# Two indexer heads as two row tiles, and scores, top-k and modulation panels in one stage

## What is computed

```python
def dsa_attend(q, iq, iw, qpos, k, v, ik, kpos, n_sel):
    dots = jnp.einsum('bqhd,bsd->bqhs', iq.astype(f32), ik.astype(f32))
    score = jnp.einsum('bqhs,bqh->bqs', jax.nn.relu(dots), iw.astype(f32))
    score = jnp.where(causal[None], score, -jnp.inf)
    top_score, idx = lax.top_k(score, n_sel)
    ...
def adaln(c, w, b):
    m = jax.nn.silu(c) @ w + b
    return jnp.split(m[:, None, :], 6, axis=-1)
```

## Time and profile before

| | |
|---|---|
| median of 3 runs | 1914.38 us (1914.14 to 1914.92) |
| the profiled execution | 1902.81 us |
| its span, first to last instruction | 1901.0 us |
| mean granted TensorE clock | 0.892 |
| TensorE busy | 1682.0 us (88%) |
| VectorE, ACT, POOL busy | 803.3 (42%), 682.4 (36%), 149.2 (8%) |
| the stages from the scores to the top-k's end | 157 to 303.4 us |

### The profile page before, as it was taken

One profiled execution on the slowest core, in us unless ns is written; L12 is line 12 of the kernel. 1 busy time (PEld: TensorE's weight loads), 2 busy tenths in 40 slices (PEclk: granted clock), 3 DMA queues, 4 the chain that ended last, 5 costly groups with the idle time before them and its releaser, 6 DMA issues.

```text
span 1901.0 us, 31118 instructions
## 1 busy us (share of the span) xinstructions
PE 1682.0 (88%) x12238; PEld 1470.6 (77%) x12238; DVE 803.3 (42%) x1736; ACT 682.4 (36%) x1228; POOL 149.2 (8%) x294
## 2 busy tenths in 40 slices
PE   4698996888988899999999776999988999998996
PEld 3484344777848799999899774778667999998995
DVE  0232286676833533333344422444334444334443
ACT  2422222333521533333332342444423433334334
POOL 0312001001110100000000031111100000000000
PEclk9695556877989899999999987889989999999998
DMA  6512183000244255444513012002341222222211
GB/s 178 184 42 62 56 288 133 23 22 0 111 177 133 67 178 177 154 159 139 159 40 128 25 57 89 23 22 110 141 154 61 89 89 88 91 87 81 78 45 45
DMA packets 154361, 189.53 MB, mean 100 GB/s; under 512 B 6789, under 2 KB 148269, under 8 KB 149974
## 3 DMA queue, kind: packets, MB, share of 16 engines
q1 hardware_dynamic: 143906, 144.65, 23.9%
q0 software_dynamic: 5600, 36.24, 5.2%
q10 hardware_dynamic: 4768, 7.42, 1.2%
HBM read 183.65 MB, written 4.83 MB: 99 GB/s over the span
## 4 chain that ended last, share of the span: by engine, by line
PE 73%; DVE 11%; issue 8%; ACT 5%; DMA 2%; ACTq 0%; DVEq 0%; POOL 0%; SPq 0%; POOLq 0%
PE ps L518 50%; PE ps L1041 3%; PE ps L1110 2%; PE ps L858 2%; PE ps L1092 2%; DVE arena L957 2%; PE ps L848 1%; DVE small L956 1%; PE ps L542 1%; PE ps L1060 1%; PE ps L601 1%; DVE arena L1271 1%; PE ps L1101 1%; PE ps L1380 1%; PE ps L1326 1%
## 5 line engine op out<-in xcount | busy, mean ns | idle before, releaser
L518 PE MATMUL ps<-hH,wH 128*128 128x260 f32 x2592 | 533.8, 287 | 59.3 <-DVE hL L669 38.8
L518 PE MATMUL ps<-hH,wL 128*128 128x260 f32 x2592 | 528.6, 286 | 0.0
L518 PE MATMUL ps<-hL,wH 128*128 128x260 f32 x2592 | 528.1, 286 | 0.0
L518 PEld LDWEIGHTS ps<-hH,wH 128*128 128x128 f32 x2592 | 406.9, 192 | 67.3 <-issue 64.6
L502 DVE TENSOR_TENSOR wL<-ring,wH 128x1024 fp32r<-128x1024 f32 (+1 forms) x172 | 203.6, 1188 | 558.8 <-ACT wH L496 558.7
L518 PEld LDWEIGHTS ps<-hH,wL 128*128 128x128 f32 x2592 | 406.3, 192 | 0.0
L518 PEld LDWEIGHTS ps<-hL,wH 128*128 128x128 f32 x2592 | 405.8, 191 | 0.0
L496 ACT ACTIVATE wH<-ring 128x1024 fp32r<-128x1024 f32 (+1 forms) x184 | 188.8, 1029 | 586.1 <-PE ps L518 573.9
L1176 ACT ACTIVATE arena<-arena 128x128 f32<-128x128 f32 (+3 forms) x128 | 72.2, 564 | 192.2 <-DVE arena L1257 107.8
L1092 PE MATMUL ps<-arena 68*128 (+4 forms) x256 | 102.7, 492 | 7.6 <-DVE arena L1157 2.6
L1110 PE MATMUL ps<-arena 128*128 (+1 forms) x640 | 93.6, 281 | 13.7 <-ACT arena L1184 13.2
(11 more groups left out here) (268 smaller groups left out, 1891.8 us busy)
## 6 DMA issues: line engine op xcount, KB each, us to landing
ring<-in_w_ada SPq DMA_DIRECT2D x48, 1024.0 KB, 8.9
ring<-in_w_up SPq DMA_DIRECT2D x44, 1024.0 KB, 5.1
ring<-in_w_down SPq DMA_DIRECT2D x16, 1024.0 KB, 5.9
ring<-in_w_in_a SPq DMA_DIRECT2D x8, 1024.0 KB, 6.8
ring<-in_w_down SPq DMA_DIRECT2D x8, 768.0 KB, 4.5
ring<-in_w_in_b SPq DMA_DIRECT2D x6, 1024.0 KB, 5.4
ring<-in_w_o_a SPq DMA_DIRECT2D x4, 1024.0 KB, 9.0
ring<-in_w_o_b SPq DMA_DIRECT2D x4, 1024.0 KB, 8.9
```

The lines of the kernel that those rows point to most:

```text
L518: ins = pe.matmul(ps[:, 2 * p + half, 0:HT], w[:, h, kc, t * P:t * P + P], mov[:, k0 + kc, half * HT:half * HT + HT], start=(first and kc ...
```

## The change

Heads are taken in pairs. An iq tile, which has two heads on its 128 partitions, is used as it is: `dve_head` writes its sum straight to `iqN`, and POOL copies only the indexer key, to both halves of `ikT`. A pair is two matmuls, on rows 0 to 63 and 64 to 127, into two PSUM banks; ACT takes the positive part of both banks in one instruction, VectorE accumulates head by head as before. The cached keys of a sample stay as the transposes leave them, even pages on partitions 0 to 63 and odd ones on 64 to 127 (one copy on ACT, of 128 x 512), and are multiplied by two matmuls of 64 rows and 64 columns. `iqz` holds all eight samples' queries, with zeros between, written once. The eight gathers are issued at the end of POOL's head stage, four into slot 1 and four into slot 2. Sample b is transposed in pair b + 2 and multiplied in pair b + 3. The new token's dots are eight matmuls of one column. ACT, no longer VectorE, copies `iwbd` and the sample scores. The two barriers that stood between the scores and the panels and the top-k are gone; TensorE waits for the sample scores' copy (`sk_scs`) before the panels. `colmask8` and its memsets are gone.

```diff
-            ("kidx", [(s, W) for s in (1, 2)], 4),
+            ("kidx", [(s, W * NS // 2) for s in (1, 2)], 1),
...
-                dve.tensor_tensor(fm[0:rows, t % 3, :], sq[0:rows, 0, :], sq[0:rows, 1, :], ALU.add).then_inc(S(f"{tag}_fm"), 1)
+                out = iqN[:, t - 5, :] if T[t][3] == "iq" else fm[0:rows, t % 3, :]
+                dve.tensor_tensor(out, sq[0:rows, 0, :], sq[0:rows, 1, :], ALU.add).then_inc(S(f"{tag}_fm"), 1)
...
-                    h = 2 * (t - 5)
-                    in_turn(pool, pool.tensor_copy(iqT[0:HD, h, :], src[0:HD, :]))
-                    ins = pool.tensor_copy(iqT[0:HD, h + 1, :], src[HD:P, :])
+                    in_turn(pool, pool.tensor_copy(ikT[0:HD, :], src[0:HD, :]))
+                    ins = pool.tensor_copy(ikT[HD:P, :], src[0:HD, :])
...
+            def turn(b):
+                s = 1 + b // 4
+                pe.wait_ge(S(full_name("kidx", s)), fill("kidx", 0, b // 4)[2])
+                pe.wait_ge(S("sk_evac"), b + 1)
                 for n in range(NPG // 2):
+                    c = b % 4 * NPG * HD + n * P
+                    ins = pe.transpose(ps[:, 4 + b % 2, n * P:n * P + P], ring[:, s, c:c + P], ident)
...
+            def dots(b):
+                pe.wait_ge(S("sk_evac"), b + 3)
+                for e in range(2):
+                    lo = HD * e
+                    ins = pe.matmul(ps[0:64, 6 + e, :], iqz[lo:lo + HD, 64 * b:64 * b + 64], ikb[lo:lo + HD, b % 2, :],
+                                    start=(b == 0), stop=(b == NS - 1))
+                ins.then_inc(S("sk_dots"), 1)
...
-            for u in range(3 * NIH):
-                qt, h = u // NIH + 1, u % NIH
-                if u >= 4:
-                    pe.wait_ge(S("sc_relu"), u - 3)
-                pe.matmul(ps[:, u % 4, 0:(qt + 1) * P], iqT[0:HD, h, qt * P:qt * P + P], ikT[0:HD, 0:(qt + 1) * P],
-                          start=True, stop=True).then_inc(S("sc_dot"), 1)
-                if u % 3 == 1:
-                    turn(u // 3)
-                if u % 3 == 2 and u >= 3:
-                    dots(u // 3 - 1)
+            for u in range(NPAIR):
+                qt, hp = u // 4 + 1, u % 4
+                w = (qt + 1) * P
+                if u >= 2:
+                    pe.wait_ge(S("sc_relu"), u - 1)
+                for o in range(2):
+                    lo = HD * o
+                    ins = pe.matmul(ps[:, 2 * (u % 2) + o, 0:w], iqN[lo:lo + HD, hp, qt * P:qt * P + P], ikT[lo:lo + HD, 0:w],
+                                    start=True, stop=True)
+                ins.then_inc(S("sc_dot"), 1)
+                if 2 <= u < 2 + NS:
+                    turn(u - 2)
+                if 3 <= u < 3 + NS:
+                    dots(u - 3)
...
+            pe.wait_ge(S("sk_scs"), 2)
...
-                act.activation(relu[:, u % 3, 0:w], ps[:, u % 4, 0:w], ACT.Relu).then_inc(S("sc_relu"), 1)
+                act.activation(relu[:, u % 2, :, 0:w], ps[:, 2 * (u % 2):2 * (u % 2) + 2, 0:w], ACT.Relu).then_inc(S("sc_relu"), 1)
...
                     pe_score(pe)
-                    phase_end(pe, "pe")
                     pe_ada(pe, "ada0b", NSC, 8)
...
                     dve_score(dve)
-                    phase_end(dve, "dve")
                     dve_topk(dve)
...
                 pool_head(pool, l)
+                if l == 0:
+                    in_turn(pool, pool.memset(iqz[:, :], 0.0))
+                    for b in range(NS):
+                        s = slot_free(pool, "kidx", 0, b // 4)
+                        gather_rows(pool, ring[:, s, b % 4 * NPG * HD:(b % 4 + 1) * NPG * HD], I["cache_kidx_a"], b).then_inc(S(full_name("kidx", s)), 16)
```

More of the change, by code:

```diff
@@ L290, in build @@
         ikws = part(72)
-        iqT = OT
+        iqN = OT[:, 0:NIH // 2, :]
         ikT = part(TOK)
@@ L698, in copied @@
         def copied(l, t):
[L699 removed]
+            return TILES[l][t][3] in ("k", "ikw")
         def upto(test, l, t):
@@ L864, in pe_score @@
-            dots(NS - 1)
-            for c in range(2):
-                pe.matmul(ps[:, 6 + c, :], zeros[0:HD, :], const[0:HD, 0:512], start=False, stop=True)
-            pe.wait_ge(S("sc_relu"), 3 * NIH)
-            pe.matmul(ps[0:64, 3, 0:NS], iqall[0:HD, 0:64], ikT[0:HD, SEQ:TOK], start=True, stop=True).then_inc(S("sk_all"), 1)
+                    c = b % 4 * NPG * HD + n * P
+                    ins = pe.transpose(ps[:, 4 + b % 2, n * P:n * P + P], ring[:, s, c:c + P], ident)
+                ins.then_inc(S("sk_turn"), 1)
@@ L889, in act_score @@
[L889 to L901 removed]
+                act.wait_ge(S("sk_turn"), b + 1)
@@ new lines, in keys @@
+                act.wait_ge(S("sk_dots"), b + 1)
+                act.activation(ikb[:, b % 2, :], ps[:, 4 + b % 2, :], ACT.Copy).then_inc(S("sk_evac"), 1)
+            for u in range(NPAIR):
+                w = (u // 4 + 2) * P
+                act.wait_ge(S("sc_dot"), u + 1)
+                if u >= 2:
+                    act.wait_ge(S("sc_acc"), 2 * u - 2)
+                act.activation(relu[:, u % 2, :, 0:w], ps[:, 2 * (u % 2):2 * (u % 2) + 2, 0:w], ACT.Relu).then_inc(S("sc_relu"), 1)
+                if 2 <= u < 2 + NS:
+                    keys(u - 2)
@@ L902, in act_score @@
+            act.wait_ge(S("sk_iwt"), 1)
+            act.activation(iwbd[0:64, :], ps[0:64, 2, 0:NS], ACT.Copy).then_inc(S("sk_iwbd"), 1)
+            act.wait_ge(S("sk_dots"), 2 + NS)
+            for e in range(2):
+                act.activation(by_token(Rsb)[:, e:NPG:2, :], ps[0:64, 6 + e, :].rearrange("p (n k) -> p n k", n=4), ACT.Relu).then_inc(S("sk_rs"), 1)
             act.wait_ge(S("sk_new"), 1)
-            act.activation(Rsb[:, PAST:PAST + 1], small[0:64, 0:1], ACT.Relu).then_inc(S("sk_rs"), 1)
+            act.activation(Rsb[:, PAST:PAST + 1], ps[0:64, 3, 0:1], ACT.Relu).then_inc(S("sk_rs"), 1)
@@ L918, in dve_score @@
+            for e in range(2):
+                for o in range(2):
+                    ins = pool.tensor_copy(diag[HD * e:HD * e + HD, :, o:NIH:2],
+                                           iqN[HD * o:HD * o + HD, :, SEQ:TOK].rearrange("p h b -> p b h"))
+                    if (e, o) != (1, 1):
+                        in_turn(pool, ins)
+            ins.then_inc(S("sk_qz"), 1)
         def dve_score(dve):
@@ L952, in dve_topk @@
                 w = (qt + 1) * P
-                scores, m8 = sc[:, qt - 1, 0:w], small[:, 0:8]
+                scores, m8 = sc[:, qt - 1, 0:w], small[:, 16:24]
                 for n in range(NSEL_P // 8):
@@ L1932, in _ @@
                 pool.sem_inc(S(name), 1)
-            pool.memset(colmask8[:, :, :], 0.0).then_inc(S("pl_z"), 1)
-            pool.wait_ge(S("pl_z"), 1)
-            for b in range(NS):
-                pool.memset(colmask8[:, b, b * NIH:b * NIH + NIH], 1.0)
             phase_end(pool, "pool")
```

94 lines of the change are left out of this document (27 added, 67 removed).

## The result

The changed kernel takes 1856.22 us (median; 1854.79 to 1860.74), the one before 1914.26 us beside it (1913.32 to 1914.92): a ratio of 0.9713, interval 0.9695 to 0.973. That is 58.0 us between the medians. The prediction was 1873.7 us, with a range that began at 1861: the sign was right, the gain was 17.5 us larger than forecast, and the range did not hold it. The profiled execution of the changed kernel took 1857.14 us, its span 1855.3 us, at a mean granted clock of 0.911 (before: 1902.81, 1901.0 and 0.892).

A forecast was written before the change was run, and what follows sets the result against it. Bound by TensorE's scores to 242 us, then VectorE's top-k, with 17.4 us lost at a barrier between. Savings of 1.4, 35.2 and 17.4, less 9.8 and 3.5, make 40.7: 1914.4 to 1873.7 us, range 1861 to 1889.

The forecast's parts named there:

- VectorE's 61.2 us top-k at once behind the last mask add: After the scores: top-k starts near 201.5, keeps its 61.2 us and ends at 262.7, 40.7 us earlier.
- the row tiles' full overlap, taken from the panels' row: Score loop: two 64-row tiles run at once, so pairs cost 15.4 us and dots 13.7.
- shape changes at 0.3 us: Score loop: 16 changes of matmul tile shape at 0.3 us each, 4.8 us in all.
- the loop's whole sum: TensorE's score loop: 42.5 us in place of 77.7, ending at 198.0 instead of 234.7.
- The 17.4 us that the sum puts down to the barrier: Between last score accumulation and top-k: removing the barrier after the sample group's scores saves 17.4 us.
- the sentence that the loop stays at a clock of 0.50: Score loop: 42 us long at granted clock 0.50, as the loop before and the panels had.
- the clock rises in the loop: Rival for the score loop: granted clock above 0.50 throughout (1852) or for a part (1863 to 1870); chance 0.09.
- The rival for a rise throughout: Score loop at half its time, 21 us, about VectorE's bound, ending 21 us earlier: 1852; within the 0.09.
- The one for a rise in a part of the loop: Clock up for only part of the score loop: 1863 to 1870 us; within the 0.09.
- The start: Score stage begins at 155.5 in place of 156.96, 1.4 us earlier, as VectorE's add writes iqN itself.
- with 7 us to spare: End of head stage: POOL's memset and eight gathers take 12 us, to 148.5, hidden behind the head stage.
- the same saving: Final sum: the 40.7 us taken off the profiled execution also come off the 1914.4 median, giving 1873.7.

The follow-up runs named there:

- The one-tile run: Changed kernel without its second row tile: odd heads' and odd pages' matmuls left out, ACT's and VectorE's work the same; 1874.65 us, one execution.
- the loop with fillers: Changed kernel with four gathers early, six top-k rounds in the loop, and unused zero-weight matmuls where TensorE waits; 1849.62 us, ratio 0.9671.

## Why the prediction was wrong

**What held.** VectorE's 61.2 us top-k at once behind the last mask add; 3.5 us from the loop's end to there (184.4 to 187.9); the row tiles' full overlap, taken from the panels' row; shape changes at 0.3 us; the panels' 52.5 us (52.3, from 192.68 to 245.0). The one-tile run, whose loop of 42.5 us stands for two tiles at 0.50, bears out the loop's whole sum; it took 1874.65 us in one execution, with the kernel before at 1910.8 beside it, where the forecast was 1873.7. An estimate from the Trainium skill's factor of 3.07 for four row tiles ("TensorE: Matmul & The Clock Gate", Part 3) would have made it 51.3; for two float32 tiles the rows show no loss. The Trainium skill, "TensorEngine Tiling (Array Packing)", Key Properties, has TensorE drained at a change of mode; the loop's sum with 0.3 us a change leaves no room for more. The 17.4 us that the sum puts down to the barrier are VectorE's gap in the kernel before; the barrier by itself was worth 8.8 us there, and in the changed kernel it opens a gap of 5 us.

**What failed** is the sentence that the loop stays at a clock of 0.50, in the part on TensorE's score loop, and with it the 0.09 for "the clock rises in the loop". From the start of the loop, 5 us at 0.50 and the rest at 1.00 make 25.5 us in place of 42.5: 17 us of the stage. The reason given against a rise was that the loop of before and the panels had both stayed at 0.50. But the loop of before uses 64 of 128 rows and does not say what two row tiles do; the sums of squares in the same rows, on 128 rows and 128 columns, had 1.00. That row was named and then given too little weight. The panels stay a puzzle: they use all 128 rows and run on four column tiles at once, and yet had 0.50 for 53 us, before and after. Their weights have 32 columns a tile, nine of them filled, and almost a third of their time goes to the turning of the rows; no run here tells which of this matters, so what decides the clock beyond the rows stays open. The Trainium skill ties the clock to how busy TensorE has been ("TensorE: Matmul & The Clock Gate", Part 1); here 98% busy on 64 rows had 0.50 and 87% on 128 rows had 1.00, so the measurement adds a condition to it. The rival for a rise throughout was priced nearly right: 21 us and "about VectorE's bound", where the loop with fillers takes 23.6. The one for a rise in a part of the loop, 1863 to 1870, was not: a rise after 5 us already saves 17 of the 21, and the range's lower end of 1861 rested on this price. The forecast less 17 us would be 1856.7, half a microsecond from the measured time; that is luck, since a start 3.4 us late and 3.8 us behind the stage cancel in it.

**The start** was 158.88 for a forecast of 155.5. POOL's twelve microseconds were called hidden "with 7 us to spare", and POOL was indeed done before the barrier; but ACT and VectorE were held until its gathers ended. TensorE's wait ahead of the rotation is 3.43 us where 1.62 is usual, so this cost 1.8 us; the rest, 1.7, was there before, since TensorE's last products of the head stage ended that much later than in the kernel before.

**The base.** The stage was 13.7 us shorter than forecast (265.4 less 251.7), which puts the forecast at 1860.0. The remaining 3.8 us lie within what the executions and the stretch behind vary by. The step "the same saving" from profiled execution to median was safe for the stage and blind behind it: before's execution was 11.6 us under its median, and a hold in layer 1's head that others have is missing in it.

## What to carry to other kernels

A change that puts more of TensorE's rows to use can lift its clock as well, so price it at both clocks, also for a rise shortly after the start, and give a row with the same rows in use more weight than the row nearest in place. Where a stage has two ends close to each other, a saving counts up to the next end only; in the kernel before the barrier was worth 17.4 us on VectorE and 8.8 us in time. And gains of 2 to 5 us ahead of a stretch whose clock goes up and down should be read in the stage and measured together, since alone they don't show in the median.

## What the runs showed of the chip

- Float32 matmuls on 64 rows kept the granted clock at 0.50 through 78 us at 98% busy; the same matmuls with zero weights on the other 64 rows, or two row tiles at once, had 1.00 from 4 to 8 us into the loop on.
- Float32 panels on four column tiles at once, with all 128 rows, stayed at 0.50 through 53 us, 51.0 of them busy.
- Two float32 row tiles of 64 rows took 3.22 us for twelve records where one took 3.18 for six (clock 0.50), and 1.07 us for four where one took 1.07 for two (clock 1.00).
- Fillers of 1.46 us in waits of 1.6 us kept the clock at 1.00 over a stretch that stood at 0.50 for 10 us without them.
- ACT and VectorE were held until 1.3 to 1.6 us after the last of a row of eight indirect gathers on POOL, and were not when four of them were issued elsewhere; ACT passed a like row in layer 1 with and without a hold.
- Executions of the same kernel differed by up to 9 us in some 1910.
